# Nine of 147 expert weight slots in three transfers instead of one

## The chip, the cores and the metric

The kernel runs on one core of a Trainium2 chip. The metric is the device time of one execution in microseconds (us). Before the change three timed runs took 2755.55, 2757.32 and 2757.51 us, so the median is 2757.32 us. A core has engines that work side by side: TensorE (PE, with its weight loads listed as PEld), VectorE (DVE), ScalarE (ACT), GpSimd (POOL), and SyncE (SP), which here issues nearly all transfers between HBM and the on-chip memory. The transfers themselves are carried by 16 DMA engines.

## The reference

The whole program is two small networks, one after the other, on 256 tokens of width 1024, in float32: four blocks (gated MLP mixers, latent attention, a gated recurrence, each with a convolved feed-forward part), then two blocks (hybrid mixers, a SwiGLU feed-forward part, and a mixture of experts). The change touches only the mixture of experts, the last large stage:

```python
logits = (hf @ w_router).astype(jnp.float32)
top_vals, top_idx = lax.top_k(logits, TOP_K)          # 2 of 8 experts for each token
gates = jax.nn.softmax(top_vals, axis=-1)
...
def expert_block(args):                               # for each block of tokens of one expert
    xb, e = args
    return (jax.nn.silu(xb @ w_gate[e]) * (xb @ w_up[e])) @ w_down[e]
```

An expert has a gate and an up matrix of 1024 x 3584 and a down matrix of 3584 x 1024. Nothing of what is computed differs between the two kernels.

## The kernel before

The experts are worked off one after another in an order by load ("ranks"). Seven ranks are written out in full (`RANKS` is 7), and a loop at the end takes what is left; in this run it goes round once. A rank's tokens are gathered into two to four units of 32 tokens. The weights of one rank arrive in 21 slots: 14 for gate and up, 7 for down. A slot is 128 partitions x 4096 float32 elements, 2 MB, that is 16 KB in each partition. I call the 16 KB of one partition a strip. The seven ranks make 147 slots, numbered 0 to 146; the loop's 21 come after them.

There are eight places in on-chip memory for slots (`slot_of`: first_slot, parts of A, HT, B, ring and UW, used in turn). SyncE goes through the slots in the order of `expert_order()`. For slot n it waits on `moe_used` until TensorE is done with the slot eight places earlier, and issues the transfer into that place (L732), which adds 16 to that place's semaphore `moe_ready`. In `slot_ready` TensorE waits on that semaphore before the first matmul of a slot (L1620 for gate and up, L1657 for down) and adds one to `moe_used` behind the last. So the transfers run as far ahead of TensorE as the eight places allow, and the order is fixed by the program text. What ScalarE and VectorE do for the experts (L2136, L3299) hangs on TensorE's products.

A short transfer elsewhere in the program matters for the prediction: L2084 (ScalarE's queue) writes eight partitions of 1 KB each out to HBM, once in each hybrid mixer.

Of the kernel before, what the change touches and what calls it, by code (L numbers as in the profile page):

```python
# [12 lines left out]
P = 128  # L13
# [34 lines left out]
SLOT = 4096  # L48
BUFFERS = 8
LOOP_BUFFERS = 7  # L50
GUEST = BUFFERS
SIDE = {
    (0, 0): [("gather", 1)], (0, 1): [("gather", 2)], (1, 0): [("flip", 0)], (0, 2): [("flip", 1)],
# [225 lines left out]
def build(nc, ins, out, stages=STAGES):  # L279
    order = program_order(stages)  # L280
    first_slab, n = {}, 0
# [4 lines left out]
    with ExitStack() as ctx:  # L286
# [3 lines left out]
        def sem(name):  # L290
            return ctx.enter_context(nc.semaphore(name))
# [119 lines left out]
        u_turned = sem("u_turned")  # L411
        moe_ready = [sem(f"moe_ready{b}") for b in range(BUFFERS)]
        guest_ready = sem("guest_ready")
        moe_used = sem("moe_used")
        up_done = sem("up_done")
        gate_done = sem("gate_done")
# [51 lines left out]
        for tile in range(ADA_FIRST, DEPTH * ADA_TILES):  # L468
            layer, t = divmod(tile, ADA_TILES)
            if layer == 0:  # L470
                b, buf, ready = ("early", tile % ADA_RING), ada_early[tile % ADA_RING], ada_ready[tile % ADA_RING]
            elif t < ADA_MIXER:
                b, buf, ready = ("late", t % ADA_DEEP), ada_late[t % ADA_DEEP], ada_ready[t % ADA_DEEP]
            elif layer == 1 and t % ADA_DEEP >= ADA_RING:
                b, buf, ready = ("wide", t % ADA_RING), ada_early[t % ADA_RING], ada_wide_ready[t % ADA_RING]
            else:
                b, buf, ready = ("mixer", t % ADA_RING), ada_mixer[t % ADA_RING], ada_mixer_ready[t % ADA_RING]
# [8 lines left out]
        def level_banks(n):  # L486
# [30 lines left out]
        slot_of = [first_slot[:, :], flat_a[:, KE * P:KE * P + SLOT], HT[:, :, :].rearrange("p a t -> p (a t)"),  # L517
                   B[:, 48:64, :].rearrange("p a t -> p (a t)"), B[:, 32:48, :].rearrange("p a t -> p (a t)"),
                   ring_flat[:, ring_order[0] * SLOT:(ring_order[0] + 1) * SLOT],
                   ring_flat[:, ring_order[1] * SLOT:(ring_order[1] + 1) * SLOT], UW[:, 0:SLOT]]  # L520
# [52 lines left out]
        def slots_before(r, c):  # L573

            if isinstance(r, int):
                return counts.slot[r, c]
            return r * SLOTS + (UP_SLOTS if c == "down" else sum(n for n, _ in UP_CHUNKS[:c]))
# [5 lines left out]
        def turn_of(n):  # L583

            return n - (n > GUEST)

        def guest(lo, hi):

            at, _, part = next(p for p in guest_parts if p[0] <= lo and hi <= p[1])
            return part[:, lo - at:hi - at]  # L590

        def loop_buffer(n):

            return (turn_of(RANKS * SLOTS) + n % LOOP_BUFFERS) % BUFFERS

        def loop_ready(r, n):

            loads = (turn_of(RANKS * SLOTS) - loop_buffer(n) + BUFFERS - 1) // BUFFERS + n // LOOP_BUFFERS + 1
            each = SLOTS // LOOP_BUFFERS
            return r * (16 * each) + 16 * (loads - each * RANKS)  # L600
# [38 lines left out]
        def _(sp):  # L639
# [16 lines left out]
            for name, use in order:  # L656
                n, tiles = SLABS[name]
                g0 = first_slab[(name, use)]
                src = ins["w_" + name]
# [41 lines left out]
            def slots(r, c, e):  # L701

                at = slots_before(r, c)
                first, count = (UP_SLOTS, DOWN_SLOTS) if c == "down" else (sum(n for n, _ in UP_CHUNKS[:c]), UP_CHUNKS[c][0])
                for j in range(count):
                    n = first + j
                    b = turn_of(at + j) % BUFFERS if isinstance(r, int) else loop_buffer(n)
                    if not isinstance(r, int):
                        sp.wait_ge(moe_used, at + (j - LOOP_BUFFERS + 1))
                    elif at + j == GUEST:  # L710
                        continue
                    elif at + j > GUEST:
                        sp.wait_ge(moe_used, at + (j - BUFFERS + (at + j > 2 * BUFFERS)))
                    elif at + j == 0:
                        continue
                    elif at + j == 4:
                        sp.wait_ge(slab_done, last_out + 1)
                    elif at + j == 5:
                        sp.wait_ge(slab_done, last_out + pair_free[ring_order[0]])
                    elif at + j == 6:  # L720
                        sp.wait_ge(slab_done, slabs_before_moe)
                    elif at + j == 7:
                        for lo, hi, part in guest_parts:
                            sp.dma_start(part, ins["w_moe_up"][GUEST, :, lo:hi]).then_inc(guest_ready, 16)
                        sp.wait_ge(u_turned, 2)
                    src = ins["w_moe_up"][e * UP_SLOTS + n] if n < UP_SLOTS else \
                        ins["w_moe_down"][e * DOWN_SLOTS + (n - UP_SLOTS)]
                    if not isinstance(r, int) and n == SLOTS - 1:
                        sp.dma_start(slot_of[b][:, 0:SLOT // 2], src[:, 0:SLOT // 2]).then_inc(half_ready, 16)
                        sp.dma_start(slot_of[b][:, SLOT // 2:SLOT], src[:, SLOT // 2:SLOT]).then_inc(moe_ready[b], 16)  # L730
                    else:
                        sp.dma_start(slot_of[b], src).then_inc(moe_ready[b], 16)  # L732

            chosen = {0: 0}
            for r, c in expert_order():
                if r not in chosen:
                    sp.wait_ge(plan_ready, 1)
                    for q in next(group for group in GROUPS if r in group):
                        if q:
                            chosen[q] = sp.value_load(plan_i[0:1, TURN[q]:TURN[q] + 1], min_val=0, max_val=EXPERTS - 1)  # L740
                slots(r, c, chosen[r])
            sp.wait_ge(plan_ready, 2)
            end = sp.value_load(plan_i[0:1, ENTRIES:ENTRIES + 1], min_val=EXPERTS, max_val=ENTRIES)
            with sp.Fori(RANKS, end) as r:
                e = sp.value_load(plan_i[0:1, bass.ds(r, 1)], min_val=0, max_val=EXPERTS - 1)
                for c in (0, 1, 2, 3, "down"):
                    slots(r, c, e)
# [39 lines left out]
        def _(pe):  # L787
# [700 lines left out]
            def moe(_):  # L1488
# [29 lines left out]
                def slot_ready(r, n):  # L1518

                    if isinstance(r, int):  # L1520
                        turn = turn_of(n)
                        if n == GUEST:
                            pe.wait_ge(guest_ready, 16 * len(guest_parts))
                        else:
                            pe.wait_ge(moe_ready[turn % BUFFERS], 16 * (turn // BUFFERS + 1))
                    else:
                        pe.wait_ge(moe_ready[loop_buffer(n)], loop_ready(r, n))

# [65 lines left out]
                def up(r, c):  # L1594
# [6 lines left out]
                    for j in range(slots):  # L1601
                        slot_ready(r, n)
                        slot = slot_of[loop_buffer(n) if loop else turn_of(n) % BUFFERS]
                        for u in range(nu):
                            if not loop and c == 0 and j == 0 and u % 2 == 0:
                                pe.wait_ge(side_taken, counts.number["gather", r, u // 2] + 1)
                            if not loop and (r, c, j, u) == (2, 0, 0, 3):
                                pe.wait_ge(y_done, 4)
                            if j == 0 and loop and c == 0 and u == 0:
                                pe.wait_ge(h_made, made_before(r, 0))  # L1610
                            elif j == 0 and loop and c:
                                pe.wait_ge(h_made, made_before(r, c - 1) + (u + 1))
                            elif j == 0 and not loop and counts.bank_made[r, c][u]:
                                pe.wait_ge(h_made, counts.bank_made[r, c][u])
                            for i in range(per):
                                k = j * per + i
                                for g in range(4):
                                    o = (4 * i + g) * width
                                    weights = guest(o, o + width) if not loop and n == GUEST else slot[:, o:o + width]
                                    last = mm(ps[u][g * UNIT:(g + 1) * UNIT, 0:width],  # L1620
                                              hg[:, u * TOK + k * UNIT:u * TOK + (k + 1) * UNIT], weights,
                                              start=(k == 0), stop=(k == KD - 1))
                            if u == nu - 1:
                                last.then_inc(moe_used, 1)
                            elif j == slots - 1:
                                last.then_inc(up_done, 1)
                        n += 1
                        if not loop and j == 1:
                            side((r, c))
# [1933 lines left out]
```

## Time and profile before

| | before |
|---|---|
| median of three runs | 2757.32 us |
| profiled execution, its own time | 2758.43 us |
| its span, first to last instruction | 2756.6 us |
| PE busy | 2694.5 us (98%) |
| DVE busy | 1529.6 us (55%) |
| moved by DMA over the span | 772.42 MB, mean 280 GB/s |

The span is divided into 40 slices of 68.9 us on the profile's page; each digit there is a busy share in tenths. The mixture of experts fills the last twelve slices. There the line for DMA stands at 9 (90% or more) and the rate at 402 to 428 GB/s in eleven slices, with 6 and 264 GB/s in the last, while the slices before these have 115 to 359 GB/s. The granted clock of TensorE stands at 9 in all slices but the last, which is 8. In the views of a shorter stretch the same two lines divide that stretch into 40 slices, and the lines under them count the packets of each queue: q1 is SyncE's, q10 is ScalarE's, q8 fetches instructions.

### The profile page before, as it was taken

How to read it: one execution, taken by the hardware profiler on the slowest of the kernel's cores; microseconds unless marked ns; L12 is line 12 of the kernel's file. 1: busy time of each engine (PE TensorE's matmuls, PEld its weight loads, DVE VectorE, ACT ScalarE, POOL GpSimd, SP SyncE). 2: the span in 40 equal slices, each digit the busy share in tenths (PEclk: the TensorE clock that was granted, in tenths of full speed). 3: DMA queues.
4: the chain of work that ended last, by engine and by line, in shares of the span. 5: the costliest groups of instructions: out<-in, count | busy, mean ns of one | idle time of the engine just before them, and what ended most of it. 6: DMA issues, size and time to landing. Idle time of an engine off the chain costs nothing.

```text
span 2756.6 us, 53880 instructions
## 1 busy us (share of the span) xinstructions
PE 2694.5 (98%) x23300; PEld 2157.6 (78%) x23300; DVE 1529.6 (55%) x3368; ACT 508.7 (18%) x1187; POOL 153.5 (6%) x248
## 2 busy tenths in 40 slices
PE   7999999999999999999999999999999999999987
PEld 6889998999998999999998899988335335742634
DVE  4548978798776997776786568665310111011001
ACT  3103304330223330112312200031001000100001
POOL 0111101210001110000100000000000000000000
PEclk9999999999999999999999999999999999999998
DMA  9779766886537877656755345556999999999996
GB/s 359 294 257 277 241 225 261 272 261 225 206 115 277 261 237 281 220 199 180 211 170 176 123 164 170 184 184 259 402 427 426 414 427 426 425 427 428 426 428 264
DMA packets 107319, 772.42 MB, mean 280 GB/s; under 512 B 11584, under 2 KB 13136, under 8 KB 51920
## 3 DMA queue, kind: packets, MB, share of 16 engines
q1 hardware_dynamic: 71920, 658.90, 62.4%
q0 software_dynamic: 35136, 110.12, 12.7%
q8 instruction: 183, 3.00, 0.4%
q14 instruction: 48, 0.39, 0.0%
q10 hardware_dynamic: 32, 0.02, 0.0%
HBM read 767.92 MB, written 1.06 MB: 279 GB/s over the span
## 4 chain that ended last, share of the span: by engine, by line
PE 87%; DMA 8%; DVE 3%; ACT 1%; issue 0%; SPq 0%; DVEq 0%; ACTq 0%
PE ps L905 17%; PE ps L916 16%; PE ps L1620 14%; PE ps L1657 7%; PE ps L808 6%; PE ps L987 3%; PE ps L1367 3%; PE ps L838 3%; DMA UW<-w_moe_up 2%; PE ps L1005 2%; PE ps L885 2%; PE ps L1482 2%; PE ps L1287 2%; PE ps L818 2%; PE ps L1101 2%; DMA B<-w_moe_down 1%
## 5 line engine op out<-in xcount | busy, mean ns | idle before, releaser
L3299 DVE TENSOR_TENSOR C<-C,ps 128x256 f32<-128x256 f32 (+1 forms) x80 | 30.7, 387 | 362.0 <-ACT C L2136 362.0
L808 PE MATMUL ps<-HT,ring 128*128 128x256 f32 x800 | 176.1, 379 | 0.0
L808 PEld LDWEIGHTS ps<-HT,ring 128*128 128x128 f32 x800 | 151.0, 190 | 20.8 <-issue 1.0
L916 PE MATMUL ps<-A,ring 128*128 128x128 f32 x1152 | 152.3, 275 | 0.0
L916 PE MATMUL ps<-A,UW 128*128 128x128 f32 x1152 | 152.2, 275 | 0.0
L916 PE MATMUL ps<-HT,ring 128*128 128x128 f32 x1152 | 152.2, 275 | 0.0
L1367 PE MATMUL ps<-HT,ring 128*128 128x256 f32 x640 | 142.5, 380 | 0.0
L916 PEld LDWEIGHTS ps<-HT,ring 128*128 128x128 f32 x1152 | 140.5, 192 | 0.2
L916 PEld LDWEIGHTS ps<-A,UW 128*128 128x128 f32 x1152 | 140.2, 192 | 0.0
L916 PEld LDWEIGHTS ps<-A,ring 128*128 128x128 f32 x1152 | 140.2, 192 | 0.0
L3323 DVE TENSOR_TENSOR X<-X,ps 128x512 f32<-128x512 f32 x24 | 16.5, 688 | 218.9 <-PE ps L1579 218.3
L1367 PEld LDWEIGHTS ps<-HT,ring 128*128 128x128 f32 x640 | 120.3, 190 | 16.9 <-issue 1.2
L905 PE MATMUL ps<-A,ring 128*128 128x128 f32 x940 | 117.0, 275 | 0.0
L2136 ACT ACTIVATE C<-ps 128x256 f32<-128x256 f32 (+1 forms) x80 | 28.5, 357 | 476.4 <-PE ps L1620 476.3
L905 PEld LDWEIGHTS ps<-A,ring 128*128 128x128 f32 x940 | 111.3, 192 | 0.3
L2479 DVE SCALAR_TENSOR_TENSOR B<-B,cact 128x1024 f32<-128x1024 f32 x88 | 105.1, 1218 | 7.7 <-DMA B<-w_ada 7.7
L987 PE MATMUL ps<-A,ring 128*128 128x256 f32 x440 | 95.8, 379 | 0.0
L1620 PE MATMUL ps<-B 128*32 128x512 f32 x848 | 93.3, 592 | 2.5 <-DMA B<-w_moe_up 2.5
L987 PEld LDWEIGHTS ps<-A,ring 128*128 128x128 f32 x440 | 83.2, 190 | 11.1
L1737 ACT ACTIVATE small<-ps,eps 128x2 f32<-128x2 f32 x12 | 3.1, 262 | 452.2 <-PE ps L1022 450.3
L762 POOL DMA_DIRECT2D ring<-w_ff_up x68 | 58.7, 863 | 434.7 <-DMA ring<-w_ff_up 434.7
L1620 PEld LDWEIGHTS ps<-B 128*32 128x32 f32 x848 | 27.3, 110 | 66.2 <-issue 61.3
(590 smaller groups left out, 5229.4 us busy)
## 6 DMA issues: line engine op xcount, KB each, us to landing
ring<-w_ff_up SPq DMA_DIRECT2D x88, 1024.0 KB, 5.6
B<-w_moe_up SPq DMA_DIRECT2D x27, 2048.0 KB, 19.9
ring<-w_moe_up SPq DMA_DIRECT2D x26, 2048.0 KB, 20.5
B<-w_ada POOLq DMA_DIRECT2D x72, 512.0 KB, 7.6
ring<-w_ff_down SPq DMA_DIRECT2D x36, 1024.0 KB, 5.0
HT<-w_moe_up SPq DMA_DIRECT2D x16, 2048.0 KB, 22.1
ring<-w_moe_down SPq DMA_DIRECT2D x16, 2048.0 KB, 23.3
ring<-w_gm_in SPq DMA_DIRECT2D x30, 1024.0 KB, 7.3
```

Source lines behind the costliest of these rows:

```text
L762: pool.dma_start(ring[:, g % RING, 2 * PAIR:3 * PAIR], ins["w_ff_up"][layer * KF + m, :, 0:PAIR], accum_op=ALU.add).then_inc(pair_added[g ...
L808: last = mm(bank[:, j * n:(j + 1) * n], ring[:, slot, k * 256 + j * P:k * 256 + j * P + P], src[:, k, :], start=(k == 0), stop=(k == KD - 1))
L818: last = mm(bank[:, j * TOK:(j + 1) * TOK], ring[:, slot, k * 256 + j * P:k * 256 + j * P + P], H[:, k, :], start=(k == 0), stop=(k == KD ...
L838: last = mm(bank[:, 0:n], ring[:, g0 % RING, o:o + P], U[:, k, 0:n], start=(k == 0), stop=(k == KD - 1))
L885: last = mm(bank, ring[:, g % RING, k * P:(k + 1) * P], src[:, kk, :], start=(kk == 0), stop=(kk == kt - 1))
L905: last = mm(bank[:, at * P:(at + 1) * P], b if by_token else a, a if by_token else b, start=(n in (0, 2) and k == 0), stop=(n in (6, 5) an ...
L916: last = mm(bank[:, at * P:(at + 1) * P], stationary[:, kind, k, :], moving(k), start=(start and k == 0), stop=(k == KD // 2 - 1), skip_gr ...
L987: last = mm(ps[2 + j][:, 0:TOK], ring[:, g % RING, k * P:(k + 1) * P], src[:, kk, :], start=(kk == 0), stop=(kk == KF - 1))
L1367: last = mm(ps[t % 4][:, j * TOK:(j + 1) * TOK], ring[:, (g0 + t) % RING, o:o + P], H[:, k, :], start=(k == 0), stop=(k == KD - 1))
L1620: last = mm(ps[u][g * UNIT:(g + 1) * UNIT, 0:width], hg[:, u * TOK + k * UNIT:u * TOK + (k + 1) * UNIT], weights, start=(k == 0), stop=(k ...
L1657: last = mm(ps[bank][g * UNIT:(g + 1) * UNIT, col:col + TOK], hidden_t(r, f, u), slot[:, i * D + g * TOK:i * D + (g + 1) * TOK], start=(f ...
L2479: return stt(out=w, in0=w, scalar=1.0, in1=cact[:, :], op0=ALU.mult, op1=ALU.mult, accum_out=mod[:, n:n + 1])
```

## The change

For the slots 45, 57, 69, 81, 93, 105, 117, 129 and 141 (`SHARED_OUT`) the one transfer of 128 partitions becomes three: partitions 0 to 111, then 112 to 119, then 120 to 127. The first adds to `moe_ready` as before. The two short ones add 16 each to a new semaphore, `low_ready`, and TensorE waits for it too before it uses such a slot.

```diff
+SHARED_OUT = range(45, 146, 12)
+WIDE = 112
...
+        low_ready = sem("low_ready")
...
                     if not isinstance(r, int) and n == SLOTS - 1:
                         sp.dma_start(slot_of[b][:, 0:SLOT // 2], src[:, 0:SLOT // 2]).then_inc(half_ready, 16)
                         sp.dma_start(slot_of[b][:, SLOT // 2:SLOT], src[:, SLOT // 2:SLOT]).then_inc(moe_ready[b], 16)
+                    elif isinstance(r, int) and at + j in SHARED_OUT:
+                        sp.dma_start(slot_of[b][0:WIDE, :], src[0:WIDE, :]).then_inc(moe_ready[b], 16)
+                        for p in range(WIDE, P, 8):
+                            sp.dma_start(slot_of[b][p:p + 8, :], src[p:p + 8, :]).then_inc(low_ready, 16)
                     else:
                         sp.dma_start(slot_of[b], src).then_inc(moe_ready[b], 16)
...
                             pe.wait_ge(moe_ready[turn % BUFFERS], 16 * (turn // BUFFERS + 1))
+                        if n in SHARED_OUT:
+                            pe.wait_ge(low_ready, 32 * (SHARED_OUT.index(n) + 1))
```

On SyncE, at slots 43 to 46 of the program before (their places are HT, two in B, and ring; the row "ISA" with moe_used is the wait for a free place):

```order
L732 DMA HT<-w_moe_up 128x4096
L732 ISA [waits moe_used]
L732 DMA B<-w_moe_up 128x4096
L732 ISA [waits moe_used]
L732 DMA B<-w_moe_up 128x4096
L732 ISA [waits moe_used]
L732 DMA ring<-w_moe_up 128x4096
```

The same place of the program after the change:

```order
L739 DMA HT<-w_moe_up 128x4096
L739 ISA [waits moe_used]
L739 DMA B<-w_moe_up 128x4096
L735 ISA [waits moe_used]
L735 DMA B<-w_moe_up 112x4096
L737 ISA
L737 DMA B<-w_moe_up 8x4096
L737 ISA
L737 DMA B<-w_moe_up 8x4096
L739 ISA [waits moe_used]
L739 DMA ring<-w_moe_up 128x4096
```

Nothing changed its place; two transfers and what sets them up stand behind the first, ahead of the next slot's.

On TensorE, the first slots that use these places, before (L1620 is the gate and up matmul; moe_ready3 to moe_ready5 belong to the places):

```order
L1620 MATMUL ps<-B 32x512 [waits moe_ready3]
L1620 MATMUL ps<-B 32x512 x31
L1620 MATMUL ps<-B 32x512 [waits moe_ready4]
L1620 MATMUL ps<-B 32x512 x31
L1620 MATMUL ps<-ring,S 32x512 [waits h_made,side_taken,moe_ready5]
```

And after:

```order
L1629 MATMUL ps<-B 32x512 [waits moe_ready3]
L1629 MATMUL ps<-B 32x512 x31
L1629 MATMUL ps<-B 32x512 [waits low_ready,moe_ready4]
L1629 MATMUL ps<-B 32x512 x31
L1629 MATMUL ps<-ring,S 32x512 [waits h_made,side_taken,moe_ready5]
```

The matmuls stand as before; the first one of the slot waits for one semaphore more.

## Rows read from the trace of the kernel before

**Rows 1.** Stretches: us, busy us of each engine (count), clock, DMA share, GB/s.
```profile
core 0: us, PE busy (x) PEld busy (x) DVE busy (x) ACT busy (x) POOL busy (x), PEclk, DMA share, GB/s
2166.00:2475.00 309.00, 307.56 (x4007) 145.84 (x4010) 32.81 (x89) 23.78 (x65) 0.00 (x0) 1.00 1.01 427
2475.00:2740.00 265.00, 234.69 (x3100) 111.57 (x3092) 27.25 (x71) 20.25 (x51) 0.00 (x0) 0.99 0.96 408
2725.00:2731.00 6.00, 4.79 (x88) 2.68 (x92) 0.00 (x0) 0.00 (x0) 0.00 (x0) 1.00 0.49 203
```

**Rows 2.** Chain that ended last, 2475 us on: start, us, what.
```profile
2475.18 30.67 DMA first_slot<-w_moe_up
...
2526.90 33.81 DMA B<-w_moe_up
...
2571.27 34.96 DMA B<-w_moe_down
...
2698.80 31.02 DMA UW<-w_moe_down
...
2729.87 7.16 PE ps L1657 x128
```

**Rows 3.** Page of DMA for 2714 to 2738 us, slices of 0.6 us.
```profile
DMA  9999999999999867655454445545544321000000
...
q1 hardware_dynamic: 555, 5.88, 58.0%
```

**Rows 4.** Page of DMA for 2158 to 2734 us: queue, packets, MB, share of 16 engines.
```profile
q1 hardware_dynamic: 16758, 241.84, 98.8%
q8 instruction: 55, 0.90, 0.6%
...
B<-w_moe_up SPq DMA_DIRECT2D x18, 2048.0 KB, 25.1
...
ring<-w_moe_down SPq DMA_DIRECT2D x12, 2048.0 KB, 29.4
```

**Rows 5.** Page of DMA for 2148 to 2160 us.
```profile
q1 hardware_dynamic: 295, 4.29, 88.4%
q8 instruction: 1, 0.02, 0.5%
...
B<-w_moe_up SPq DMA_DIRECT2D x2, 2048.0 KB, 9.2
```

**Rows 6.** Page of DMA for 1830.3 to 1830.6 us, slices of 7.5 ns: L2084's transfer.
```profile
GB/s 0 0 0 0 0 0 0 0 0 0 273 137 0 0 137 1 0 0 0 137 137 1 0 1 137 137 0 0 0 0 1 1 0 0 1 0 0 0 0 0
DMA packets 16, 0.01 MB, mean 27 GB/s; under 512 B 8, under 2 KB 16, under 8 KB 16
...
q10 hardware_dynamic: 16, 0.01, 12.6%
```

**Rows 7.** Issues of line 732: duration ns min/median/max.
```profile
L732 SPq DMA_DIRECT2D B<-w_moe_up x27: 328/333/885, 1894.1 to 2650.1; - x27
```

## Prediction

> **What bounds the kernel now.** I read the busy shares of two stretches of the expert stage first, then the chain that ended last, then the DMA page of the last microseconds. From 2166 to 2475 us TensorE is busy 307.56 of 309 us, and the transfers run at 427 GB/s with a share of 1.01: both are full, and TensorE sets the pace. From 2475 to 2740 us TensorE is busy 234.69 of 265 us, so 30.3 us idle, and the transfers are still full [rows 1]. The chain shows what it waits for: from 2475 us it is made of transfers of 30.7 to 35.0 us, each of which is mostly the queue ahead of it, up to the last piece, a slot landing at 2729.83 us followed by 7.16 us of matmuls [rows 2]. So in the last 260 us the end is set by the time at which the DMA engines have carried all slots. Whatever moves that moment moves the end by as much, as long as it moves it by less than the 30.3 us that TensorE has idle, or moves it later.
>
> All 16 engines together give 427 GB/s, so one gives 26.7, and a strip of 16,384 bytes takes it 0.61 us; a slot of 8 strips for each engine takes 4.91 us. The engines don't end together. In slices of 0.6 us the share stays at 9 up to 2721.8, falls to 5 by 2724.2, stays at 4 or 5 up to 2732.6 and is 0 from 2734.4 us on [rows 3]; between 2725 and 2731 us it is 0.49 [rows 1]. That is eight engines done by about 2724.5 us and eight that go on to 2734.4: a lead of 9.9 us. What holds back the late ones can be read from the queues: 55 instruction fetches (q8) took 0.6% of 16 engines over 576 us, some 55 us of engine time [rows 4]; if these fall on eight engines and cost them a little over their own time, the lead is accounted for. The eight were last level near 2152 us: from 2148 to 2160 us the queues are dry for a moment (88.4 and 0.5% busy, a slot landing 9.2 us after its issue [rows 5], against 25.1 and 29.4 us later [rows 4]). The 11.1% missing there is 21.3 us of engine time, 2.7 us for each of the eight early ones.
>
> **The change, part by part.** *The wide transfer.* 112 strips on 16 engines are 7 for each, 4.30 us instead of 4.91. *The short ones.* Eight strips on eight engines, twice: 2 strips more for these eight. Together they have 9 strips in such a slot, the other eight have 7; per slot +0.61 and -0.61 us, over nine slots +5.5 and -5.5 us. If the eight are the early ones and every strip takes 0.61 us, the late ones end at 2728.9 us. The early ones would end at 2724.5 + 5.5 - 0.6 = 2729.4 us, since slot 45 lies ahead of the dry moment, which swallows its 0.6. The last landing is then 5.0 us earlier. That is the plain sum.
>
> But it takes for granted that eight engines writing to eight neighbouring partitions are as fast as sixteen writing to 128. The program has one kind of transfer of that form, read where the change writes: L2084's, eight partitions of 1 KB. Its 16 packets, eight of them under 512 B (one completion for each of eight engines), took 12.6% of 16 engines over 0.3 us, which is 0.605 us for 8,192 bytes: 13.5 GB/s per busy engine, half of the 26.7. From the slice of the first packet (75 ns) to that of the last completion (at most 262 ns) pass 187 ns, so 44 GB/s for all eight together, 1.65 engines' worth, starting up and completions included [rows 6]. No row shows a long write of this form, so I bound it: at best 0.61 us for a short transfer of 128 KB (full speed), at half speed 1.21 us, at 44 GB/s 2.98 us. I take 2.45 us, which is two engines' worth (53.4 GB/s), the value next to the 44 of the nearest row if its start is taken out of it. Less than 0.61 us is excluded by the 26.7 GB/s of an engine in streaming, over which no row goes.
>
> With 2.45 us the eight engines need 4.30 + 4.91 = 9.21 us for such a slot instead of 4.91, which is 4.30 more; nine times 38.7 us. Off that go the 2.7 us that they stood dry behind slot 45 anyway, and their lead of 9.9 us: they end 26.1 us after 2734.4. The other eight get done 5.5 us earlier and wait for nothing, but every slot needs both. The end moves by +26.1 us.
>
> The Trainium skill has a rule on this that speaks against the change: SBUF — State Buffer, section "Door 1: The DMA port swizzle (why [64,N] ≈ [32,N])", says that four neighbouring partitions share one port of the memory, that a transfer gets as many ports as its partitions reach, and that 0..3 alone gave 27.6 GB/s. By it partitions 112 to 119 reach two ports, and 128 KB would take about 2.4 us, an estimate from that page; those two ports also have engines of their own in mid-stream. Rows 6 go along with it, but for reads of 1 KB only.
>
> *The other edits.* SyncE issues two more transfers per slot at 0.333 us each [rows 7], 0.67 us; a slot lands 25 to 29 us after its issue [rows 4], and that queue hides it. If it did not, it would be 9 x 0.67 = 6 us. The short ones stand in SyncE's queue ahead of the next slot's strips, which on these eight engines start later by what was counted above. TensorE's added wait (`low_ready`) sits on a matmul that waits for the same slot anyway. Behind it are all further matmuls, and for them ScalarE, VectorE and SyncE's wait for a free place. In the stretch up to 2475 us the transfers are 25 to 29 us from issue to landing with eight places ahead, so a first late slot costs TensorE nothing; once the sum passes its margin it idles there instead of at the end, and the total stays that of the engines.
>
> Against the profiled execution (2758.43 us, 1.8 of it outside the span) the forecast is 2784.5 us. That execution lies 1.1 us over the median of the runs, so 2783.4 us on the median's scale.
>
> **The rivals.**
> *It works as written* (plain sum): short transfers at full speed, eight early engines. For it: the lead of 9.9 us is there, and nine slots of 1.2 us difference fit it almost exactly. Against it: rows 6. -5.0 us, 2752 us.
> *The short transfers cost half speed only:* 2 x 1.21 + 4.30 - 4.91 = 1.82 us per slot, 16.3 in all, of which the dry moment swallows 1.8 and the lead 9.9: +4.6 us, 2762 us. With 2.98 us instead: 5.35 per slot, 48.2 - 2.7 - 9.9 = +35.6 us, 2793 us. These two are the ends of my forecast's own case.
> *The wide transfer is slowed too.* 7 strips for each engine no longer fall on the bounds of the memory that 8 per engine fell on, so engines could meet in it as well. No row has 112 partitions. If its strips went at 13.5 GB/s, 7 x (1.21 - 0.61) = 4.2 us per slot come on top, 37.8 us: +64 us, 2821 us.
> *The eight are the late ones.* No row tells engines apart by number. Full speed: +5.5 us, 2763 us; at 2.45 us per short transfer +38.7 us, 2796 us, without any lead to take off. Against it: the change gives more to eight and less to eight, which is of use only for the early ones, but nothing in the trace says which they are.
>
> The Trainium skill says for such queues (DMA: Bandwidth & Descriptors, section "Why a DMA increments its semaphore by 16 and not by 1") that a transfer uses the largest count up to 16 that divides its outer size, and the lowest-numbered engines of the core. Rows 6 agree on eight for eight partitions; which eight are early no row here shows.
>
> **How the numbers follow.** Short transfers slowed, wide ones not: 0.45 (2762 to 2793 us, my forecast 2783). Works as written: 0.26. Wide ones slowed too: 0.19. The late eight: 0.10. The range goes from 2751 us, a microsecond under the plain sum, to 2822 us, where the third case stands; some 15% are left out, nearly all above. A measurement of this kernel tells about 0.2%, 5.5 us, from no change. The plain sum, 5.0 us, lies just at that bound: half of its chance, 0.13, is faster, the other half is the same; with 0.04 from the lower end of the first case and the late eight at full speed, the same gets 0.17. Slower: 0.70.
>
> **What would show it.** In the changed profile the short transfers have a landing of their own: if the gap from the wide one's landing to theirs is about 5 us more than one would expect from two strips, the forecast's mechanism is there. The two-step fall of the DMA share at the end should vanish or turn round, with the last landing near 2760 us, the rate from 2166 to 2475 us should lie under 427 GB/s, and TensorE should wait for transfers before 2475 us. If instead both groups of engines end within a microsecond near 2729 us at 427 GB/s, the plain sum was right. A rate that falls while 112 partitions are in flight, with no short transfer there, speaks for the third case. If the lead at the end has grown to some 20 us, the eight were the late ones. The forecast is wrong if the last landing is before 2734 us.

## The result, and the profile after

The changed kernel takes 2886.85 us (median of 4 runs, 2886.35 to 2898.21); the kernel before, run beside it, 2756.44 us (4 runs). The ratio is 1.0479, with a 95% interval of 1.0467 to 1.0491: 130 us or 4.8% slower. The forecast was 2783 us, with a range that ended at 2822. The sign was right, the size was not.

The first view is again the one by stretches, of the kernel after; it answers to [rows 1].

```profile
core 0: us, PE busy (x) PEld busy (x) DVE busy (x) ACT busy (x) POOL busy (x), PEclk, DMA share, GB/s
2110.00:2166.00 56.00, 54.89 (x660) 24.21 (x656) 5.83 (x12) 6.03 (x16) 0.00 (x0) 1.00 1.01 353
2166.00:2475.00 309.00, 258.75 (x3311) 118.98 (x3303) 23.86 (x72) 18.86 (x52) 0.00 (x0) 0.97 1.01 354
2475.00:2740.00 265.00, 204.01 (x2384) 83.77 (x2388) 19.53 (x49) 14.63 (x40) 0.00 (x0) 0.92 1.00 340
2740.00:2866.00 126.00, 106.65 (x1390) 51.85 (x1385) 13.96 (x34) 8.61 (x19) 0.00 (x0) 0.99 0.83 348
```

Read the last two columns together. The DMA share is 1.01 as before, but the rate has fallen from 427 to 354 GB/s. The engines are not waiting for work; strips take longer, and the time in which they are held up counts as busy: in the trace's list of DMA packets 99% of the strips of this stretch took under 0.7 us before, and now 19% take more than 0.9, half of these more than 1.2. A share near 1 alone would have shown nothing. TensorE now idles 50.3 us in the stretch from 2166 to 2475 us, in which it was full before. Its granted clock, a mean over its two levels of 2.4 and 1.2 GHz, is 0.97 in this stretch and 0.92 in the next, in which it idles 61 us; the transfers are busy throughout and set the end, so I take the clock for a consequence.

The rate carries the whole sum. At 427 GB/s the bytes of the four stretches would have taken less time by 56 x (1 - 353/427) = 9.7, 309 x (1 - 354/427) = 52.8, 265 x (1 - 340/427) = 54.0 and 126 x (1 - 348/427) = 23.3 us, together 139.8. Reckoned in the same way the kernel before lost 2.4 us around its dry moment (409 GB/s over 58 us from 2110) and some 6.5 us from there to 2734.4, where its transfers end. The difference is 131 us, and the chain of waits of the kernel after ends by as much later: its last slot lands at 2861.27 us, in place of 2729.83 [rows 2]. The lines are start, duration in us, and what.

```profile
2796.87 30.30 DMA UW<-w_moe_up
...
2831.17 30.10 DMA UW<-w_moe_down
...
2861.32 7.16 PE ps L1666 x128
```

The page of DMA for 2158 to 2866 us, in 40 slices of 17.7 us, shows where the rate goes; it answers to [rows 4].

```profile
GB/s 427 340 214 427 428 353 213 417 428 365 218 375 426 373 231 342 426 386 218 346 401 362 245 381 366 427 256 394 332 391 287 392 293 235 428 430 429 428 422 83
...
q1 hardware_dynamic: 17147, 245.64, 96.6%
q8 instruction: 57, 0.93, 0.6%
...
ring<-w_moe_up SPq DMA_DIRECT2D x18, 2048.0 KB, 40.1
B<-w_moe_up SPq DMA_DIRECT2D x16, 2048.0 KB, 38.7
ring<-w_moe_down SPq DMA_DIRECT2D x12, 2048.0 KB, 43.4
```

Between the first shared slots the rate is 417 to 428, as before. In the first three dips it falls to 213 to 218: half. Later dips are mostly shallower in a slice, but longer. Landings have gone from 25 to 29 us up to about 40. The last view is the page of DMA for 2830 to 2870 us, in slices of 1 us, for the tail of [rows 3].

```profile
GB/s 434 426 393 410 459 410 426 459 426 410 442 426 410 426 377 410 434 426 401 303 139 49 66 33 66 66 33 66 57 41 41 41 57 49 41 33 0 0 0 0
```

Before, half of the engines ran on alone for 9.9 us. Now the rate falls within 3 us to 33 to 66 GB/s, about two engines' worth at 26.7, and stays there for some 15 us. Fourteen engines end together, two come later.

### The profile page after: what moved, and what is told of

It is laid out like the page before. It is cut to its first block, busy times and chain, and to the rows that moved or that the text cites. A ratio compares the mean times of both kernels' runs of the same rounds, so it can differ in the third digit from the quotient of the medians.

```text
span 2885.5 us, 53940 instructions
## 1 busy us (share of the span) xinstructions
PE 2720.0 (94%) x23300; PEld 2153.0 (75%) x23300; DVE 1530.5 (53%) x3368; ACT 508.8 (18%) x1187; POOL 153.5 (5%) x248
## 3 DMA queue, kind: packets, MB, share of 16 engines
q0 software_dynamic: 35136, 110.12, 12.3%
## 4 chain that ended last, share of the span: by engine, by line
PE 76%; DMA 18%; DVE 4%; ACT 1%; issue 1%; another core or an unknown queue 1%; SPq 0%; DVEq 0%; ACTq 0%
PE ps L912 16%; PE ps L923 15%; PE ps L1629 9%; PE ps L815 6%; PE ps L1666 5%; DMA first_slot<-w_moe_up 4%; DMA UW<-w_moe_down 4%; DMA UW<-w_moe_up 4%; PE ps L994 3%; DMA B<-w_moe_up 3%; PE ps L1374 3%; PE ps L845 2%; PE ps L1012 2%; PE ps L892 2%; PE ps L1489 2%; PE ps L1294 2%
## 5 line engine op out<-in xcount | busy, mean ns | idle before, releaser
L1629 PE MATMUL ps<-ring,B 128*32 128x512 f32 (+1 forms) x768 | 72.7, 531 | 10.7 <-DMA ring<-w_moe_up 10.7
```

What stands on the lines that cost most here:

```text
L1629: last = mm(ps[u][g * UNIT:(g + 1) * UNIT, 0:width], hg[:, u * TOK + k * UNIT:u * TOK + (k + 1) * UNIT], weights, start=(k == 0), stop=(k ...
```

## The experiments

Each run stands beside one of the kernel before on the same chip (2757.6 to 2760.2 us). All change only how the nine shared slots (or those named) are loaded, with the waits to match. "Rate" is that from 2166 to 2475 us.

| the nine slots as | us | rate, GB/s |
|---|---|---|
| 112 + 16 partitions | 2896.11 | 355 |
| seven times 16 at steps of eight, two of 8 | 2898.85 | 358 |
| 0 to 63, 64 to 127 | 2880.95 | 359 |
| even, odd | 2757.87 | 427 |
| 112 only | 2864.46 | 356 |
| the two short ones only | 2765.36 | 399 |
| 64 + 32 + 8 + 8 + 16, 9 and 7 strips | 2774.50 | 418 |
| 64 + 32 + 32 at steps of two and four | 2756.53 | 427 |

**Which part of the change costs?** First the short transfers were replaced by one of 16 partitions.

```diff
-for p in range(WIDE, P, 8):
-    sp.dma_start(slot_of[b][p:p + 8, :], src[p:p + 8, :]).then_inc(low_ready, 16)
+sp.dma_start(slot_of[b][WIDE:P, :], src[WIDE:P, :]).then_inc(low_ready, 16)
```

> The nine slots come as 112 partitions and one transfer of 16 partitions; no transfer of 8 partitions is left. Theory 1 (place: a strip is slow when its engine writes partitions that another engine writes at that moment, which the 112 partitions bring about because seven strips an engine run over the boundaries of the eight that each has in a full slot): the strips of the 112 still take 1.2 to 1.4 us for 0.615, and the run stays at 2840 to 2890 us. Theory 2 (the price is in the short transfers, as forecast): sixteen engines take one strip each, at most 2.45 us for 0.61, nine times 1.84 us less the 9.9 us lead of eight engines: 2755 to 2775 us. Theory 3 (any split of a slot costs, by the number of its transfers): two in place of three, half of the 130 us: about 2820 us.

It took 2896 us, six above the range of the place theory. That is against my forecast's theory (2755 to 2775), in which the eight-engine form was the cost. Then each part was loaded alone.

```diff
 sp.dma_start(slot_of[b][0:WIDE, :], src[0:WIDE, :]).then_inc(moe_ready[b], 16)
-for p in range(WIDE, P, 8):
-    sp.dma_start(slot_of[b][p:p + 8, :], src[p:p + 8, :]).then_inc(low_ready, 16)
```

> Of the nine slots only the 112 partitions are loaded, in one transfer; the last 16 partitions keep old data, and an eighth of these slots' work for the transfers is left out (nine times 0.61 us of 16 engines). Place theory (what counts is which partitions are written at the same time): the 112 partitions, seven strips an engine, meet each other and the strips of the next slots still take 1.1 to 1.4 us; 2800 to 2870 us, and the part of the changed kernel's 130 us that is missing belongs to the short transfers. Short-transfer theory (my forecast): the wide transfer is as fast as written, 427 GB/s throughout, and the end comes 5.5 us sooner than before: 2752 us.

```diff
-sp.dma_start(slot_of[b][0:WIDE, :], src[0:WIDE, :]).then_inc(moe_ready[b], 16)
-for p in range(WIDE, P, 8):
-    sp.dma_start(slot_of[b][p:p + 8, :], src[p:p + 8, :]).then_inc(low_ready, 16)
+sp.dma_start(slot_of[b][WIDE:WIDE + 8, :], src[WIDE:WIDE + 8, :]).then_inc(moe_ready[b], 16)
+sp.dma_start(slot_of[b][WIDE + 8:P, :], src[WIDE + 8:P, :]).then_inc(low_ready, 16)
```

> Of the nine slots only the last 16 partitions are loaded, in the two transfers of 8 partitions; the other 112 keep old data, so nine times 4.30 us of 16 engines' work is left out. If a short transfer takes no longer than its strips (0.61 us), the transfers run ahead by nine times 3.7 us and TensorE alone sets the end, 2728 us. At the forecast's 2.45 us each, a shared slot takes the eight engines 4.9 us, as much as a whole slot before, so they end where they ended before less the 2.7 and 9.9 us counted there: 2735 to 2758 us. Place theory: as the forecast for these eight, but the engines that own the partitions wait as well, so strips of 1.2 us and more also appear in the neighbouring slots: 2740 to 2790 us.

The wide transfer by itself took 2864 us, 104 us over the kernel before, though an eighth of these slots isn't moved. These are its stretches; the share is 1.01 and 1.00 at 356 and 347 GB/s, the picture of the full change.

```profile
2166.00:2475.00 309.00, 274.59 (x3570) 121.57 (x3562) 25.83 (x74) 18.86 (x52) 0.00 (x0) 0.97 1.01 356
2475.00:2740.00 265.00, 216.74 (x2468) 93.62 (x2472) 21.09 (x52) 14.63 (x40) 0.00 (x0) 0.90 1.00 347
```

With the short transfers alone the run took 2765.36 us, above the 2735 to 2758 of my forecast and within the 2740 to 2790 of the place theory, though seven eighths of nine slots aren't moved. The last slot in the chain of waits of this run:

```profile
2703.61 31.70 DMA UW<-w_moe_down
```

It lands at 2735.31, 5.5 us later than in [rows 2]. Where the time goes can be read from the trace's semaphore updates, which tell when each of the 16 engines had landed its part of a transfer. From slot 81 to 141 the last landing of the second short transfer comes 2.4 to 2.5 us after the last landing of the slot ahead, so a short one takes the engine that is last there some 1.2 us. Where the engines stood closer together, at slot 57, the first five landings of the second come 2.2 us after those of the first. The rest is lost in whole slots: the last landing of slot 80 comes 8.84 us after that of slot 79, in place of 4.89.

The same updates in the changed kernel show the parts side by side. In the nine shared slots the last landing of the wide transfer comes 8.7 to 10.1 us after that of the slot ahead, in place of the 4.30 of the forecast. The last landing of the two short ones comes 0.2 us before it at slot 45, 3.2 and 2.5 us after it at slots 57 and 69, and 1.9 to 2.0 us after it from slot 81 on, in place of 4.90. So the wide transfer is the costly part. By itself it costs about 110 us (104, and the 5.5 of the strips left out) of the 130.

**What makes a strip slow: the place, or being split?**

```diff
+sp.dma_start(slot_of[b][0:64, :], src[0:64, :]).then_inc(moe_ready[b], 16)
+sp.dma_start(slot_of[b][64:P, :], src[64:P, :]).then_inc(low_ready, 16)
```

> The nine slots come as partitions 0 to 63 and 64 to 127, one transfer each. Theory 1 (place): with four strips to an engine, two engines write into the same eight partitions throughout, so the slot's strips take about 1.23 us for 0.615: 4.9 us a slot, 44 us over nine, 2795 to 2810 us, more if the slots behind suffer too. Theory 2 (short transfers): none here, 2751 to 2760 us. Theory 3 (number of transfers): about 2820 us.

```diff
+sp.dma_start(slot_of[b][0:P:2, :], src[0:P:2, :]).then_inc(moe_ready[b], 16)
+sp.dma_start(slot_of[b][1:P:2, :], src[1:P:2, :]).then_inc(low_ready, 16)
```

> The nine slots come as the even partitions and the odd ones, 64 each: the same count, sizes and strips an engine as with the two halves, but an engine's four strips lie in eight partitions that no other engine writes. Theory 1 (place): strips of 0.615 us, 2751 to 2760 us. Theory 2 (short transfers): the same, 2751 to 2760 us. Theory 3 (number of transfers): as with the two halves, about 2820 us.

The two have the same number of transfers, bytes and strips. One took 2880.95 us, the other 2757.87. Their stretch from 2166 us, first the halves, then every other partition:

```profile
2166.00:2475.00 309.00, 262.88 (x3378) 117.92 (x3370) 25.83 (x74) 18.86 (x52) 0.00 (x0) 0.98 1.01 359
```

```profile
2166.00:2475.00 309.00, 307.57 (x4008) 145.92 (x4008) 32.87 (x89) 23.85 (x65) 0.00 (x0) 1.00 1.01 427
```

So neither a split nor a count of 64 costs anything by itself; which partitions a transfer holds does. The halves cost 122 us, though, against the 44 (2795 to 2810 us) that I expected. But the two also read different rows, so reading and writing were then crossed.

```diff
+sp.dma_start(slot_of[b][0:64, :], src[0:P:2, :]).then_inc(moe_ready[b], 16)
+sp.dma_start(slot_of[b][64:P, :], src[1:P:2, :]).then_inc(low_ready, 16)
```

> As with the two halves, the nine slots are written to partitions 0 to 63 and 64 to 127, but the rows that are read are every other one (so a slot's rows lie in another order than the reference wants). If the place that is written makes the strips slow, as with the two halves: 2881 us, 359 GB/s from 2166 to 2475 us. If the rows that are read do it (sixteen engines reading within one half of a slot's 2 MB), as with every other partition: 2758 us, 427 GB/s.

```diff
+sp.dma_start(slot_of[b][0:P:2, :], src[0:64, :]).then_inc(moe_ready[b], 16)
+sp.dma_start(slot_of[b][1:P:2, :], src[64:P, :]).then_inc(low_ready, 16)
```

> The counterpart: every other partition is written, from the first and the second 64 rows of the slot (again another order of rows than the reference wants). If the place that is written decides: 2758 us, 427 GB/s. If the rows that are read decide: 2881 us, 359 GB/s.

Halves written, every other row read: 2883.87 us. Every other partition written, halves read: 2760.95 us. The same stretch of the two, in this order:

```profile
2166.00:2475.00 309.00, 262.68 (x3360) 119.22 (x3352) 25.46 (x74) 18.91 (x52) 0.00 (x0) 0.97 1.01 356
```

```profile
2166.00:2475.00 309.00, 307.57 (x4004) 145.68 (x4000) 32.83 (x89) 23.83 (x65) 0.00 (x0) 1.00 1.01 427
```

The written side decides: the two runs repeat the halves and the every other partition within 0.2%.

**Which places?**

```diff
+for k in range(6):
+    sp.dma_start(slot_of[b][k:P:8, :], src[k:P:8, :]).then_inc(low_ready, 16)
+sp.dma_start(slot_of[b][6:P:8, :], src[6:P:8, :]).then_inc(moe_ready[b], 16)
+for p in (7, 71):
+    sp.dma_start(slot_of[b][p:p + 57:8, :], src[p:p + 57:8, :]).then_inc(low_ready, 16)
```

> The nine slots come as seven transfers of 16 partitions, each taking one partition out of every eight (0, 8, 16, ... then 1, 9, 17, ...), and the last partition of every eight in two transfers of 8 partitions. Each engine has as many strips as in the changed kernel (nine for eight engines, seven for the others), but in the seven transfers none shares its eight partitions with another. Theory 1 (place): strips take 0.615 us again, rate back to 427 GB/s; only the second short transfer meets another engine (at most 0.6 us a slot): 2745 to 2770 us. Theory 2 (any 8-partition transfer is slow): +4.3 us a slot on eight engines less the lead, 2770 to 2795 us. Theory 3 (number of transfers): nine for three a slot, at least as slow as the changed kernel, 2880 us or more.

2898.85 us: the place theory missed here, and the theory of numbers, refuted by every other partition a moment ago, hit. What had been wrong was my map: I had taken an engine's place to be eight neighbouring partitions. The Trainium skill (SBUF — State Buffer, section "Door 1: The DMA port swizzle (why [64,N] ≈ [32,N])") gives another: four neighbours share a port with the four that stand 32 further, so partitions 0 to 63 reach eight of sixteen ports, and so do 0, 8, 16, ... 120. Both ran at half rate in their first dips (220 and 216 GB/s), every other partition at full rate (427). The runs agree with that map in every form whose ports can be counted like this; they show places, not ports. Two forms were then chosen by it.

```diff
+sp.dma_start(slot_of[b][0:P:2, :], src[0:P:2, :]).then_inc(moe_ready[b], 16)
+for rows in (slice(1, P, 4), slice(3, P, 4)):
+    sp.dma_start(slot_of[b][rows, :], src[rows, :]).then_inc(low_ready, 16)
```

> The nine slots come as the even partitions (64), every fourth from 1 (32) and every fourth from 3 (32): three transfers as in the changed kernel, eight strips for every engine as before. Port map: 32 partitions at steps of four reach all sixteen ports with two partitions each, so 2751 to 2760 us, as before. If a step over the partitions or fewer than 64 of them cost something, as the seven transfers of 16 partitions at steps of eight (2899 us) might be read, it stands between 2800 and 2900 us.

```diff
+sp.dma_start(slot_of[b][0:P:2, :], src[0:P:2, :]).then_inc(moe_ready[b], 16)
+for rows in (slice(1, P, 4), slice(3, 32, 4), slice(35, 64, 4), slice(67, P, 4)):
+    sp.dma_start(slot_of[b][rows, :], src[rows, :]).then_inc(low_ready, 16)
```

> The nine slots come in five transfers that give eight engines nine strips and the others seven, as the change meant: the even partitions (64), every fourth from 1 (32), eight partitions 3, 7, ... 31, eight partitions 35, 39, ... 63, and sixteen partitions 67, 71, ... 127. Place theory with the Trainium skill's port map: the first four reach for each engine only the port that it has in a whole slot, so their strips stay at 0.61 us; in the last, two engines meet at a port for one strip (1.2 us for 0.6). No slow stretches behind them; 2750 to 2765 us, below 2757 if the eight with nine strips are the ones that were done early, above if they are the late ones. Theory that transfers of 8 partitions are slow by their count: two of them a slot, +38.7 us less 12.6, about 2784 us. Theory that the number of transfers counts: 2880 us or more, as with nine strided ones.

Three transfers that respect the map cost nothing (2756.53 us, 427 GB/s). The one with nine strips for eight engines and seven for the others took 2774.50 us: 14 us slower, nine above the range expected. Its stretch:

```profile
2166.00:2475.00 309.00, 303.16 (x3942) 143.83 (x3938) 31.12 (x85) 23.07 (x63) 0.00 (x0) 0.99 1.01 418
```

309 x (1 - 418/427) = 6.5 us are lost there, to the last 16 partitions, where engines meet: the next run leaves just these out and has 426 GB/s. That was allowed for only in part. The other reason is the next one.

**Which eight engines are early?**

```diff
+sp.dma_start(slot_of[b][0:P:2, :], src[0:P:2, :]).then_inc(moe_ready[b], 16)
+for rows in (slice(1, P, 4), slice(3, 32, 4), slice(35, 64, 4)):
+    sp.dma_start(slot_of[b][rows, :], src[rows, :]).then_inc(low_ready, 16)
```

> Nine slots as even partitions (64), every fourth from 1 (32), and two transfers of 8 partitions (3, 7, ... 31 and 35, 39, ... 63); the partitions 67, 71, ... 127 are left out and keep old data. Eight engines have eight strips a slot as before, the other eight six. By the port map no engine meets another: strips stay at 0.61 us and no slow stretch is seen, though there are two transfers of 8 partitions in each slot. It also tells which eight are late: if the late ones are those with six strips, they gain nine times 1.22 us, 11 us, both groups end within 2 us of each other near 2724 us and the run takes about 2748 us; if the late ones are those with eight, the end stays at 2734 us (2758 us), and the lead grows from 10 to 21 us. If transfers of 8 partitions are slow whatever they write: +4.3 us a slot for the eight, 2770 to 2800 us.

2754.85 us, which is neither 2748 nor 2758, though 2758 is too near for the time of one run to decide. The rate is 426 GB/s from 2166 to 2475 us, so two transfers of 8 partitions a slot cost nothing where they respect the map. The end, in slices of 1.25 us from 2690 to 2740 us:

```profile
GB/s 433 433 433 433 419 419 419 433 419 459 419 419 419 406 433 419 439 433 419 433 406 328 360 374 321 164 72 52 39 39 59 52 26 20 0 0 0 0 0 0
```

Engines with six strips save 9 x 1.22 = 11 us. A late one among them would end at 2734.4 - 11 = 2723.4, an early one with eight strips still at 2724.5: together one step down. That step is there, at 2720 to 2723. But before it two engines' worth are missing from about 2716 us on (328 to 374 GB/s, 12.3 to 14 engines), and after it two engines' worth (39 to 59 GB/s) run on to 2732. So two of the late engines are among the eight that the short transfers use, and two of the early ones are not. The semaphore updates of slot 141 agree: the last six landings of its short group (2600.8 to 2602.3 us) are three from each of two engines, which so carry short transfers, and all others are in by 2596.1. The chain's last slot starts at 2695.71 and lands 31.69 us later, at 2727.40, only 2.4 us ahead of [rows 2].

```profile
2695.71 31.69 DMA UW<-w_moe_down
```

**Why 14 us a slot?** The first dip of the full change loses 9.7 us (up to 2166 us), and a later stretch of twelve slots' time 59 x (1 - 324/427) = 14.2 us:

```profile
2466.00:2525.00 59.00, 38.02 (x496) 18.95 (x492) 2.75 (x4) 3.34 (x9) 0.00 (x0) 0.86 1.01 324
```

Counted by the mean landing of the whole slots halfway between the shared ones, the third to the ninth cost 12.3, 13.4, 13.8, 14.1, 15.2, 12.5 and 12.6 us. Much of this falls on whole slots. From slot 116 to 128 the last landing falls behind by 14.6 us, of which 6.5 are in the shared slot 117 (9.5 and 1.9 us for 4.89) and 8.1 in the eleven whole ones behind it. Then one shared slot by itself, and nine in a row:

```diff
-SHARED_OUT = range(45, 146, 12)
+SHARED_OUT = range(81, 82)
```

> Only one slot, number 81, is loaded in the changed manner. If the nine prices are equal and independent, one ninth of the changed kernel's 131 us: +14.6 us, 2772 us. If a slot's price grows with how far the engines have come apart before it (which the earlier shared slots cause), the single one is cheaper: in the changed kernel the first of the nine put the landings of the next whole slots back by about 10 us; +8 to +11 us, 2765 to 2768 us. If the price is only the strips of that slot itself at half rate (4.3 us for the wide transfer and at most 4.3 for the short ones), +4 to +9 us, 2761 to 2766 us.

```diff
-SHARED_OUT = range(45, 146, 12)
+SHARED_OUT = range(45, 54)
```

> The nine shared slots stand in a row, 45 to 53, in place of every twelfth (with a semaphore each for their short transfers). If the price is that of each slot by itself, +130 us as in the changed kernel: about 2887 us, 14.6 us a slot. If most of it is paid by the whole slots beside a shared one (engines that have come apart meet an engine that is still or already in another slot), nine in a row have that border once and not nine times: nine times some 8.6 us inside, and one border of 5 to 10 us: 2830 to 2845 us.

The single slot took 2764.64 us (6 runs; ratio 1.003, interval 1.0018 to 1.0043), 6.4 us. Its rate over 59 us, twelve slots' time:

```profile
2280.00:2339.00 59.00, 55.83 (x871) 29.71 (x863) 9.52 (x33) 3.75 (x12) 0.00 (x0) 1.00 1.01 365
```

59 x (1 - 365/427) = 8.6 us are lost, which the interval of the ratio (5 to 12 us) holds. The 8.6 us fit the last two cases of the expectation alike. But the whole slot ahead pays too: the last landing of slot 80 comes 8.58 us after that of slot 79, in place of 4.89. Nine in a row took 2812.89 us, 55 us over before and below both ranges expected. The page of DMA, 2100 to 2240 us in slices of 3.5 us:

```profile
GB/s 407 435 440 431 403 290 201 201 220 211 211 201 225 225 220 225 218 225 220 220 215 220 229 220 225 229 225 197 220 234 229 225 229 234 286 435 426 421 431 435
```

A flat floor at about 220 GB/s, 8.2 engines' worth: a shared slot among shared ones takes twice the time of a whole one, 2.1 MB at 220 GB/s in 9.5 us for 4.9. So what one slot standing alone costs beyond 4.6 us seems to be paid where engines in a shared slot meet engines in a whole one. That should grow as they come apart, which the last run was to test.

```diff
+SHARED_OUT = range(117, 118)
+FEWER = range(45, 114, 4)
```

The slots of `FEWER` are loaded as in the run on the early engines.

> One slot, number 117, is loaded in the changed manner. Ahead of it, in every fourth slot from 45 to 113, the partitions 67, 71, ... 127 are left out and the rest comes in transfers in which no engine meets another, so that eight engines have eight strips and the others six: when slot 117 comes, the engines stand some 20 us apart, and not 3 us as at slot 81 of the run with one shared slot. If apartness sets the price (each engine crosses the others' whole slots for longer), the transfers lose 11 to 14 us around slot 117, as around the later slots of the changed kernel. If it does not, they lose 7 to 8 us, as the single slot did. The time itself: the run with nine such slots and no shared one took 2755 us, so 2762 us without the effect, 2766 to 2770 us with it.

It took 2773.44 us, above the 2766 to 2770 expected. Around slot 117:

```profile
2452.00:2511.00 59.00, 48.18 (x408) 13.52 (x400) 6.55 (x17) 2.68 (x7) 0.00 (x0) 0.91 1.01 313
```

59 x (1 - 313/427) = 15.8 us lost, for the 8.6 of the same slot form in a stream whose engines were close. The 20 us of the expectation was too high: by the semaphore updates the 16 landings of slots 112 and 113 lie 9.4 and 10.4 us apart, against 3.1 us at slot 79 of the run with one shared slot. Slot 45 of the change uses the same place in memory as slot 117; its dip cost 9.7 us with 4.8 us between the landings of slot 43, so it isn't the place. Engines that are further apart thus make the same slot dearer, in this one run by 1.8 times.

## Why the prediction was wrong

- **That the end is set by the last landing, and moves with it:** right. The chain ends in transfers, and the 131 us by which the chain's last slot lands later is the 130 us of the result.
- **The direction:** right, but in part by luck. The short transfers were to bring the loss; on the engines that end last they took less than half of what was forecast.
- **The plain sum:** wrong for two reasons. Strips didn't keep their 0.61 us, and the eight that do the short transfers are not the eight early ones. Two of them are late, so nine slots of 0.61 us more would have put 5.5 us onto the end, even at full speed throughout. A gain was not to be had from it. The rival of the late eight had this price, for eight engines where two are enough.
- **The short transfers at 2.45 us:** too dear for the engines that set the end. Both together end 1.9 to 2.0 us after the wide one from slot 81 on, in place of 4.90; loaded alone, 1.2 us each, and up to 2.2 us where engines stood close. The form was not the reason: eight partitions at steps of four cost nothing.
- **The wide transfer at 4.30 us:** the step that failed. The sum took its strips at full speed, and the rival in which they are not had 0.19. In the change its last landing comes 8.7 to 10.1 us after the slot ahead, and a run with it alone is 104 us slower. The prediction named the mechanism, that seven strips an engine don't fall on the bounds that eight fell on, but priced only the short transfers, to which it also held the Trainium skill's port rule. That rule, which counts the ports that a transfer's partitions reach, would not have warned of the wide one: 112 partitions reach all sixteen. What the runs add is that the slowdown also comes where each engine leaves its own place. No run loads 112 partitions in one transfer that keeps to the places, so that the count of 112 plays no part is inferred from the other forms.
- **The size of that rival, 4.2 us a slot and +64 us in all:** too small. Inside a run of shared slots the price is 4.6 us for the whole of a slot, near the 4.2 that this rival put on the wide transfer. What it left out is the whole slots next to a shared one: 8.6 us lost by a single slot, and 9.7 rising to 14 and 15 in the change. The engines come apart there: ahead of the nine shared slots the 16 landings of one slot lie 4.8, 6, 10, 18, 27, 33, 29, 32 and 32 us apart, nearly all of it two engines, while the other fourteen stay within 2 to 9 us. The last run speaks for this as the reason of the rise; why it is two engines that fall behind stays open.
- **SyncE's issues and TensorE's added wait at nothing:** nothing in the runs speaks against it. Three transfers for one cost nothing when the places are right.
- **What would show it:** the rate under 427 and TensorE waiting for transfers before 2475 us came as said. These didn't tell the forecast from the rival. The sign that does is the gap from the wide transfer's last landing to that of the short ones: the forecast asked for about 6 us (1.2 for two strips, and 5 more), and it is 3.2 us at most. So the forecast's mechanism is not what made the change slow.

No version tried beats the kernel before by more than can be measured: the best, the three transfers at steps of two and four, is within 0.2% of it. After the halves, in which every engine has eight strips, one engine's worth of transfers (26 GB/s from 2842 to 2858 us) still runs on alone; what holds it back was not settled.

## What to carry to other kernels

A stream like this one, in which each engine keeps to its own place, loses half its rate while a transfer breaks the pattern, and the whole transfers beside it pay as well; so split by steps that keep every engine in its place, and try one such transfer by itself before nine. Watch the bytes per second and not the busy share, which stayed at 1 here. Before shifting work from late engines to early ones, show which engines a transfer uses and which are late, with a run that only takes work away.

## What the runs showed that I had not expected

- The same 2 MB written in two transfers of 64 partitions cost 122 us more over nine slots if neighbours go together and nothing if every other partition does; the side that is read doesn't matter (2883.87 against 2760.95 us when crossed).
- A split slot costs nothing by itself: three transfers for one ran at 427 GB/s.
- One form of transfer has prices from 4.6 us (in a row of its like) over 8.6 (alone) to 15.8 us (between engines that have come apart).
